# Where the top-k rounds of an indexer stand in VectorE's queue: six rounds move from behind the latent norms to late steps

## The reference

```python
def dsa_attention(q, k, v, iq, ik, iw, t5_table):
    topk = min(TOPK_MAX, S // 4)                       # 128
    def block(bi):                                     # 128 queries
        logits = jnp.einsum('bthd,bsd->bths', iqb, ik).astype(jnp.float32)
        score = jnp.einsum('bth,bths->bts', iwb, jax.nn.relu(logits))
        adm = (kpos[None, :] // CHUNK) <= (qpos[:, None] // CHUNK)
        score = jnp.where(adm[None], score, -jnp.inf)
        _, sel = lax.top_k(score, topk)
        ...                                            # attention over the selected keys
```

## Time and profile before

| what | before |
|---|---|
| median of three runs | 3366.16 us (3365.66 to 3366.56) |
| profiled execution, its own time | 3365.66 us |
| its span, first to last instruction | 3363.8 us |
| PE busy | 3233.6 us, 96% of the span |
| DVE, ACT, POOL busy | 49%, 40%, 41% |
| mean granted TensorE clock | 0.992 |
| the 29 steps, first layer | about 2142 to 2290 us of the span |
| the same, second layer | 651.8 us later |

### The profile page before, as it was taken

How to read it: one execution, slowest core, us unless ns; L and a number is a source line. 1 busy time by engine, 2 the same in 40 slices (tenths; PEclk the granted TensorE clock), 3 DMA queues, 4 the chain that set the end, 5 groups by cost and what they waited for, 6 DMA issues and landing times. The chain is left out here.

```text
span 3363.8 us, 46345 instructions
## 1 busy us (share of the span) xinstructions
PE 3233.6 (96%) x16177; PEld 2576.3 (77%) x16177; DVE 1643.3 (49%) x2609; ACT 1351.7 (40%) x2110; POOL 1375.7 (41%) x694
## 2 busy tenths in 40 slices
PE   7999999999998999999999999999999989999998
PEld 5677777788886677777788887767888867778887
DVE  5843335665635743335755633773333238533332
ACT  5755554322225755555322224454222234532222
POOL 2233333444443233333444444534444435444444
PEclk8999999999999999999999999999999999999999
DMA  3122221255532122222245533212222232023232
GB/s 130 56 79 80 83 78 63 81 180 194 212 106 72 56 79 80 82 78 68 83 175 195 210 107 103 76 32 72 97 96 99 97 112 76 32 76 100 94 104 102
DMA packets 94332, 335.82 MB, mean 100 GB/s; under 512 B 11236, under 2 KB 12132, under 8 KB 93968
## 3 DMA queue, kind: packets, MB, share of 16 engines
q1 hardware_dynamic: 92640, 328.12, 28.6%
q10 hardware_dynamic: 1584, 6.29, 0.5%
HBM read 332.22 MB, written 8.44 MB: 101 GB/s over the span
## 5 line engine op out<-in xcount | busy, mean ns | idle before, releaser
L434 POOL TENSOR_TENSOR wLo<-wring,wHi 128x1024 fp32r<-128x1024 f32 x482 | 1172.0, 2431 | 1770.2 <-ACT wHi L414 1770.0
L458 PE MATMUL psG<-hHi,wHi 128*128 128x512 f32 x2992 | 1181.7, 395 | 10.0 <-ACT whole L1817 4.0
L458 PE MATMUL psG<-hLo,wHi 128*128 128x512 f32 x2992 | 1169.8, 391 | 11.1 <-POOL hLo L483 10.2
L458 PE MATMUL psG<-hHi,wLo 128*128 128x512 f32 x2992 | 1165.7, 390 | 0.0
L414 ACT ACTIVATE wHi<-wring 128x1024 fp32r<-128x1024 f32 x482 | 511.0, 1060 | 976.9 <-PE psG L458 956.4
L458 PEld LDWEIGHTS psG<-hHi,wHi 128*128 128x128 f32 x2992 | 562.1, 188 | 149.8 <-issue 25.8
L458 PEld LDWEIGHTS psG<-hLo,wHi 128*128 128x128 f32 x2992 | 561.9, 188 | 142.7 <-POOL hLo L483 24.9
L458 PEld LDWEIGHTS psG<-hHi,wLo 128*128 128x128 f32 x2992 | 562.4, 188 | 114.1 <-issue 0.5
L458 PE MATMUL psG<-hidLo,wHi 128*128 128x512 f32 x704 | 273.9, 389 | 0.0
L458 PE MATMUL psG<-hidHi,wHi 128*128 128x512 f32 x704 | 273.9, 389 | 0.0
L458 PE MATMUL psG<-hidHi,wLo 128*128 128x512 f32 x704 | 273.9, 389 | 0.0
(11 more groups left out here) (323 smaller groups left out, 3476.4 us busy)
## 6 DMA issues: line engine op xcount, KB each, us to landing
wring<-in_w SPq DMA_DIRECT2D x494, 512.0 KB, 3.3
modw<-in_wmod SPq DMA_DIRECT2D x96, 512.0 KB, 5.3
e_copies<-e_rows ACTq DMA_DIRECT2D x8, 512.0 KB
T_tab<-e_copies SPq DMA_DIRECT2D x4, 1024.0 KB, 5.5
mask<-in_mask SPq DMA_DIRECT2D x2, 1536.0 KB, 6.2
xin_sb<-in_x SPq DMA_DIRECT2D x4, 512.0 KB, 5.1
e_copies<-e_rows ACTq DMA_DIRECT2D x8, 256.0 KB
out<-o_sb SPq DMA_DIRECT2D x4, 512.0 KB, 3.8
```

What stands on the lines that cost most here:

```text
L434: pool.tensor_tensor(wLo[:, c % CUTS, :, :], wring[:, c % RING, :, :], wHi[:, c % CUTS, :, :], ALU.subtract).then_inc(w_cut[c % CUTS], 1)
L458: mm = pe.matmul(psG[:, G.slot(u), :], w[:, c % CUTS, k, :], r(j), start=start and j == 0 and n == 0, stop=stop and j == len(kts) - 1 and ...
```

## The change

The number of rounds stays 48 and so does their order. They are spread anew over DVE's queue: one fewer ahead of step 0, one fewer each at steps 0 and 2, none at the two places inside step 8 (there were 2 and 4), one at step 8 behind `lowest(8)`, and 2, 2, 2, 1 and 1 at steps 11 to 15, where there were none.

| step | first | 0 | 1 | 2 | 3 | 4 | 5 | 6 | 7 | 8, inside | 8 | 9 | 10 | 11 | 12 | 13 | 14 | 15 |
|---|---|---|---|---|---|---|---|---|---|---|---|---|---|---|---|---|---|---|
| before | 9 | 5 | 4 | 5 | 4 | 4 | 1 | 1 | 3 | 2 + 4 | 0 | 4 | 2 | 0 | 0 | 0 | 0 | 0 |
| changed | 8 | 4 | 4 | 4 | 4 | 4 | 1 | 1 | 3 | 0 | 1 | 4 | 2 | 2 | 2 | 2 | 1 | 1 |

```diff
-TAKEN_FIRST = 9
-TAKE_AT = {0: 5, 1: 4, 2: 5, 3: 4, 4: 4, 5: 1, 6: 1, 7: 3, 9: 4, 10: 2}
-TAKEN_LATENT = (2, 4)
+TAKEN_FIRST = 8
+TAKE_AT = {**{n: 4 for n in (0, 1, 2, 3, 4, 9)}, 7: 3, **{n: 2 for n in range(10, 14)}, **{n: 1 for n in (5, 6, 8, 14, 15)}}
...
                             dve.wait_ge(z2_full, 4)
                             dve.sem_inc(T.emptied(tr["SK"]), 1)
-                            takes(TAKEN_LATENT[0])
                             dve.wait_ge(d_full, 2)
...
                             dve.tensor_tensor(qr[:, :], sq[:, 0, :], sq[:, 1, :], ALU.add).then_inc(z2_full, 1)
-                            takes(TAKEN_LATENT[1])
...
-                        takes(TAKE_AT.get(s, 0))
+                        for _ in range(TAKE_AT.get(s, 0)):
+                            take(taken)
+                            taken += 1
                         if s in DONE_AT:
                             mix(DONE_AT[s])
```

More of the change, by code:

```diff
@@ L2180, in mix @@
                                                  var[:, n:n + 1]).then_inc(var_full, 1)
[L2182 to L2186, removed]
                     for s in range(STEPS + 1):
```

## The result

| | before | changed |
|---|---|---|
| median | 3366.07 us (3364.49 to 3369.65, 6 runs) | 3384.6 us (3380.51 to 3387.84, 6 runs) |
| ratio, 95% interval | 1 | 1.0053 (1.004 to 1.0066) |
| span of the profiled execution | 3363.8 us | 3385.4 us |
| mean granted TensorE clock | 0.992 | 0.985 |

The forecast was 3375.8 us, with a range up to 3381. In the changed file every line behind the table has a number lower by one, so L458 is L457 and L1650 is L1649; L2164 is L2163, L2179 is L2178, L2113 is L2112, and the scaling L2196 is L2189.

The account below looks back on a forecast made before the run. PE, busy for 96% of the span, was taken to bound the kernel. Per layer 5.9 us lost less 1.1 gained, 9.6 us for two layers, on 3365.66 us profiled, plus 0.5 for the median: 3375.8 us, range 3370.5 to 3381.

Parts of the forecast that it names:

- A round at 1.517 us: DVE's time for one top-k round of 512 keys, read from the timeline before.
- step 8's six for nothing: Taking the six rounds out of step 8 saves nothing, since DVE idles there for PE anyway.
- the ninth behind `lowest(8)` for nothing: The single round put at step 8 costs nothing: 2.80 us of DVE idle time behind step 9's rounds absorbs it.
- The gain at step 8: Changed round widths at steps 5 to 7 bring the latents' scaling earlier, shortening PE's wait at `turn(6)`: 1.1 us per layer.
- the third rival: No gain at step 8: squaring and mask both wait POOL out, the loss stands alone, 3378 us; chance 0.22.
- The delay of 5.9 us per layer: Steps 11 to 15: eight late rounds, 12.1 us, less 5.2 us DVE idle time and 0.97 us PE slack.
- The sum, 9.6 us: Whole kernel: 5.9 us lost less 1.1 us gained, 4.8 us per layer, for two layers.
- a rival of 0.05: The clock falls at steps 11 to 15 as PE idles more: 5 us more per layer, 3386 us; chance 0.05.
- What was to be seen: Signs in the profile after: clock 1.00, `scores(12)` to `scores(17)` about 25.2 us, new PE waits of 5 to 7 us together.

Follow-up runs that it names:

- e5: The changed kernel with 18 small filler matmuls per layer ahead of PE's waits for DVE at steps 12 to 17: 3373.56 us.
- e9: The kernel before with three rounds moved from inside step 8 to steps 11, 12 and 13, one each: 3370.71 us.
- e4: The kernel before with one of step 7's three rounds moved to step 9: 3364.89 us.
- e3: The kernel before with only the six rounds inside step 8 moved, two each to steps 11, 12 and 13: 3384.76 us.
- e8: The kernel before with small filler matmuls in three waits that PE has anyway, at steps 8, 9 and 11: 3365.93 us.

## Why the prediction was wrong

- *A round at 1.517 us, step 8's six for nothing, the ninth behind `lowest(8)` for nothing:* right. No new wait before step 12 in the profile after.
- *The gain at step 8, 1.1 us per layer:* 1.09 us. Its working held too: the squaring got through between two instructions of POOL (0.63 us), the mask cost 0.87 us where 0.7 was taken. The Trainium skill (page "SBUF — State Buffer", section "SBUF: two separate sides") has a port pair that is held for a whole instruction; the trace doesn't contradict it, but between two instructions of POOL, back to back in its queue, DVE came in, so the third rival with its bound of -0.1 us is out. One reading behind the bounds was loose: of the mask's times in the earlier trace rows, 0.29 us is that over 256 keys and 0.43 that over 512; for 384 keys, the one that was moved, no row shows an undisturbed time. It changes nothing in the sum.
- *The delay of 5.9 us per layer:* 5.7 us with the clock held (e5). There DVE had no wait at all from `lowest(11)` to the end of `lowest(16)`, as the forecast had it; in the changed kernel itself only up to `lowest(14)`, for behind it DVE waits for the slow PE.
- *The sum, 9.6 us, and the time that it gives:* e5, which has the change's work and delay and a clock of 0.990 to 0.993, took 3373.6 us, 2.2 us under the forecast. Of these, 2 x 0.34 us are the wait of `values(8)`, a gain that the sum left out, and 2 x 0.2 us the delay.
- **The step that failed** is the clock, which the sum holds at full speed and so puts at nothing, with a rival of 0.05 beside it: "Against it: the gaps are 1 to 2 us each, not one long one." The gaps were shorter still, 0.3 to 1.24 us, and the clock fell behind them, in both layers of both profiles of the changed kernel. The term that was put at 0 measured 7.8 and 4.3 us in the two layers. The rival had it at 5 us per layer and 3386 us; 3384.6 was measured. That the rival's time came so near is in part luck. Its 11 us of lost work were about right (10.2 in the first layer), but it let the slow stretch hide all 5.9 us of waits, where 2.5 were hidden, and the rest of the sum was 2.2 us too high. The row that the rival rested on, 67% busy at 0.68, pointed the right way; it was set aside for the shape of the gaps, for which no row spoke. The range ended at 3381, short of this rival, though it was worked out.
- *What was to be seen:* "the clock at 1.00" was wrong; "`scores(12)` to `scores(17)` at about 25.2 us" was right only with the waits filled; the new waits were 3.7 us together and not 5 to 7, for the slow PE swallowed the rest.

What stays open: what amount of idle time, in which spacing, tips the clock. The same waits do not always do it. 1.71 and 0.27 us at step 8 tipped it in the second layer of e9 and not in the first; 0.57 and 0.27 us tipped it in the second layer of e4 and not in the first; in the changed kernel the fall came during or behind the third of the new waits, or behind the fourth. No run varied the spacing alone.

## What to carry to other kernels

Where work moves on a helper engine's queue, look up the idle time at both places: the six rounds were free inside step 8, and at steps 11 to 13 they cost 18 us (e3), with a fall of the clock in both layers. When a change makes TensorE wait in a stretch of small products, count its lost time once for the wait and expect it again for the clock; then compare a version with fillers in the waits, which tells the two apart. A kernel whose executions scatter by 10 us at differing clocks may already stand at that edge.

## What the runs showed of the hardware

- Short waits are enough to lower TensorE's clock. Four waits of 0.31 to 1.24 us, 3.2 us in all, stood ahead of about 20 us at 1.2 GHz in one layer. The Trainium skill, page "TensorE: Matmul & The Clock Gate", section "A second HAM failure mode: psum-queue depth-cycling", says of another kernel that frequent short idling between groups of matmuls makes the clock go up and down. The traces here agree in that short waits do it; they show one fall per layer and not a swing.
- TensorE was busy for all of the 15 us from 2245 on, at a clock of 0.62: a busy engine can be a slow one, and a table of waits shows nothing of it (from `scores(14)` at 2237.05 to `scores(20)` at 2267 us there are none). Only the granted clock and the duration of one instruction show it.
- The kernel before, with not a line changed, had a mean clock of 0.989 or less in 30 of 88 executions, and these took 5 to 16 us more than 3365.5 us, the median of the other 58. With the fillers of e8 none of twelve executions was as long.
